# The up product of a gated feed-forward block by Strassen's scheme, on one Trainium2 core

## The chip, the cores and the metric

The kernel runs on one core of a Trainium2 chip. Its time is the device time of one execution in microseconds, given as the median of three runs. Five engines run side by side, each with its own instruction queue that it works off in order: TensorE (PE, with its weight loads as PEld), VectorE (DVE), ScalarE (ACT), GpSimd (POOL) and SyncE (SP, which here only issues DMAs). They meet in semaphores.

## The reference, cut to what matters

A trunk of two layers is applied to two sequences (prompt and sample) of 256 tokens, width 1024, in float32. Each layer has an attention mixer with two kinds of heads, a layer norm, and then the part that is changed, a gated feed-forward block with a convolution along the tokens:

```python
def conv_glu(x, w_up, conv_w, conv_b, w_down):      # D_FF = 2816, w_up: 1024 x 5632
    S = x.shape[1]
    g, v = jnp.split(x @ w_up, 2, axis=-1)
    gp = jnp.pad(g, ((0, 0), (1, 1), (0, 0)))
    g = gp[:, :S] * conv_w[0] + gp[:, 1:S + 1] * conv_w[1] + gp[:, 2:S + 2] * conv_w[2] + conv_b
    return (jax.nn.gelu(g) * v) @ w_down

# in encoder_trunk, for each layer:
x = layer_norm(ALPHA * x + mix, ln1_g[i], ln1_b[i])
ffn = conv_glu(x, w_up[i], conv_w[i], conv_b[i], w_down[i])
gate = jax.nn.sigmoid(x @ w_ple_gate[i] + b_ple_gate[i])
x = layer_norm(ALPHA * x + ffn + gate * (p[i] @ w_ple[i]), ln2_g[i], ln2_b[i])
```

## The kernel before

All 512 tokens (256 of the prompt, then 256 of the sample) are held at once. To get float32 accuracy out of a matmul with shortened operands, every operand is split into a high part (a copy into the short format, by ScalarE) and a low part (the value minus its high part, by GpSimd for weights and by VectorE for activations), and each product is three matmuls, hi x hi, hi x lo and lo x hi, added up in PSUM (`product`, lines 1238 to 1242). Each matmul has its own weight load. PSUM is eight banks of 512 columns, `ps[:, bank, :]`.

Weights come as a stream of blocks of 128 x 1024. SP loads a block into one of two slots of `raw`; ScalarE writes `w_hi` (`hi`, line 646), GpSimd writes `w_lo` (`lo`, line 535), in a ring of eight slots; TensorE uses it. SP may load the next block into a raw slot when GpSimd has finished with it (`w_split`), and ScalarE may overwrite a slot of the ring when TensorE has used it (`w_used`).

Around the change a layer goes as follows. The gate product (`w_ple_gate`, eight groups of 24 matmuls) ends; then TensorE runs the up loop. Its 22 tiles are of 128 gate and 128 value columns of `w_up` each. For a tile, `up_tile` runs the gate half and then the value half, 8 k-steps x 3 matmuls with 512 token columns each, into two banks:

```python
for v in range(2):
    pe.wait_ge(w_split.sem, w_split.at(layer, s[0] + v - AHEAD + 1) + s[1])
    a = slot(s[0] + v, KD)
    for k in range(KD):
        ins = product(ps[:, bank + v, :], (a[0][:, k, :], a[1][:, k, :]), (xt_hi[:, k, :], xt_lo[:, k, :]),
                      k == 0, k == KD - 1)
```

Behind it ScalarE takes the centre tap of the convolution (`conv_centre`, line 756), VectorE adds the two side taps (`conv_sides`, lines 1120 and 1123), ScalarE applies GELU (line 762) and VectorE multiplies with the value half (`glu`, line 1129). The result goes to `hbuf` (16 tiles) or `late` (the last six, split into `s_hi` and `s_lo` at once, lines 853 and 1198). The first 16 tiles run in hardware loops on all engines (`Fori`), the last six are written out. Then the down product: its first group (tile 16) makes one block of 6 matmuls for each of the four token blocks, into the banks of `DOWN_BANK`, and the other tiles follow, with their split in step (lines 858 and 1202).

The order of the work on every engine is written out by hand; a waiting instruction holds everything behind it on its engine.

## Time and profile before

| | |
|---|---|
| median of three runs | 1203.26 us (1203.0 to 1203.35) |
| the profiled execution: span from first to last instruction | 1201.6 us |
| TensorE busy | 1187.7 us (99%), 5784 matmuls |
| weight loads busy | 972.2 us (81%) |
| VectorE, ScalarE, GpSimd busy | 522.3 us (43%), 483.7 us (40%), 585.3 us (49%) |
| mean granted clock of TensorE | 0.996 |
| DMA | 113.45 MB, 94 GB/s over the span |

The profiled execution's own time is its span and what lies around it; the median of the runs is 1.66 us above the span. Busy times of matmuls overlap, as one starts before the record of the one ahead of it ends, so the length of a stage is read from starts and not from the sum of the records.

### The profile page before, as it was taken

The numbers are of one execution on the slowest core, as the hardware profiler recorded it, in microseconds if no ns is written. First come the engines' busy times: TensorE is split into PE (matmuls) and PEld (weight loads), VectorE is DVE, ScalarE is ACT, GpSimd is POOL, SyncE is SP. The second block draws the span as 40 slices with busy tenths as digits, with TensorE's granted clock in tenths as the row PEclk, the third lists the DMA queues.
The fourth block names the chain that finished last, engine by engine and source line by source line (L and its number), as shares of the span: only waits on it lengthen the run. The fifth ranks groups of instructions, "written<-read, shape, count | busy, mean of one in ns | idle before, by whom it ended". The sixth has DMA issues, their size and how long they took to land.

```text
span 1201.6 us, 16482 instructions
## 1 busy us (share of the span) xinstructions
PE 1187.7 (99%) x5784; PEld 972.2 (81%) x5784; DVE 522.3 (43%) x1094; ACT 483.7 (40%) x890; POOL 585.3 (49%) x338
## 2 busy tenths in 40 slices
PE   8999999999999999999999999999999999999997
PEld 6887778888888888888888777788888888888886
DVE  7777857522122134211587787474221122441107
ACT  3456763344334333323144767433443333332310
POOL 6665854465444444344264756634644444434330
PEclk9999999999999999999999999999999999999999
DMA  6321222344323332223132202433433333223311
GB/s 224 87 78 46 89 59 100 127 135 124 105 87 89 103 106 90 86 93 104 53 88 71 81 26 71 140 105 88 140 109 101 103 89 99 94 75 101 105 35 70
DMA packets 121754, 113.45 MB, mean 94 GB/s; under 512 B 6753, under 2 KB 97889, under 8 KB 121697
## 3 DMA queue, kind: packets, MB, share of 16 engines
q1 hardware_dynamic: 121696, 112.71, 30.3%
q8 instruction: 33, 0.54, 0.2%
q14 instruction: 25, 0.20, 0.1%
HBM read 110.60 MB, written 2.10 MB: 94 GB/s over the span
## 4 chain that ended last, share of the span: by engine, by line
PE 97%; DVE 1%; POOL 1%; DMA 1%; DVEq 1%; issue 0%; SPq 0%
PE ps L1240 29%; PE ps L1241 29%; PE ps L1242 29%; PE ps L1406 3%; PE ps L1392 3%; PE ps L1380 1%; PE ps L1382 1%; PE ps L1250 1%; PE ps L1363 1%; DMA x<-in_x_prompt_dram 1%; POOL w_lo L545 1%; DVEq L887 0%; POOL ln_r L541 0%; PE ps L1417 0%; DVE bn L1222 0%; PE ps L1462 0%
## 5 line engine op out<-in xcount | busy, mean ns | idle before, releaser
L535 POOL TENSOR_TENSOR w_lo<-raw,w_hi 128x1024 fp32r<-128x1024 f32 x188 | 453.1, 2412 | 404.7 <-ACT w_hi L646 404.5
L1240 PE MATMUL ps<-xt_hi,w_hi 128*128 128x512 f32 x704 | 273.9, 389 | 0.0
L1241 PE MATMUL ps<-xt_lo,w_hi 128*128 128x512 f32 x704 | 273.9, 389 | 0.0
L1242 PE MATMUL ps<-xt_hi,w_lo 128*128 128x512 f32 x704 | 273.9, 389 | 0.0
L646 ACT ACTIVATE w_hi<-raw 128x1024 fp32r<-128x1024 f32 x188 | 197.8, 1055 | 132.6 <-PE ps L1242 63.0
L1240 PE MATMUL ps<-w_hi,stat 128*128 128x512 f32 x480 | 187.8, 391 | 0.0
L1241 PE MATMUL ps<-w_lo,stat 128*128 128x512 f32 x480 | 187.1, 390 | 0.0
L1242 PE MATMUL ps<-w_hi,stat 128*128 128x512 f32 x480 | 187.0, 390 | 0.0
L1240 PEld LDWEIGHTS ps<-xt_hi,w_hi 128*128 128x128 f32 x704 | 132.1, 188 | 27.7
L1242 PEld LDWEIGHTS ps<-xt_hi,w_lo 128*128 128x128 f32 x704 | 132.1, 188 | 27.4
L1241 PEld LDWEIGHTS ps<-xt_lo,w_hi 128*128 128x128 f32 x704 | 132.1, 188 | 27.2
L1240 PE MATMUL ps<-w_hi,xt_hi 128*128 128x512 f32 x352 | 141.5, 402 | 2.3 <-POOL w_lo L545 2.1
L1242 PE MATMUL ps<-w_hi,xt_lo 128*128 128x512 f32 x352 | 138.4, 393 | 0.0
L1241 PE MATMUL ps<-w_lo,xt_hi 128*128 128x512 f32 x352 | 138.1, 392 | 0.0
L1120 DVE SCALAR_TENSOR_TENSOR hbuf<-ps,cols,hbuf 128x510 f32 x32 | 24.0, 749 | 189.3 <-ACT hbuf L756 189.3
L1242 PEld LDWEIGHTS ps<-w_hi,stat 128*128 128x128 f32 x480 | 90.1, 188 | 19.2
L1240 PEld LDWEIGHTS ps<-w_hi,stat 128*128 128x128 f32 x480 | 90.1, 188 | 18.1 <-POOL w_lo L535 0.8
L1241 PEld LDWEIGHTS ps<-w_lo,stat 128*128 128x128 f32 x480 | 90.2, 188 | 17.1
L1202 DVE TENSOR_TENSOR stat<-hbuf,stat 128x512 fp32r<-128x512 f32 x32 | 22.2, 693 | 140.1 <-ACT stat L858 140.1
L1240 PEld LDWEIGHTS ps<-w_hi,xt_hi 128*128 128x128 f32 x352 | 66.6, 189 | 16.7 <-POOL w_lo L545 3.6
L1242 PEld LDWEIGHTS ps<-w_hi,xt_lo 128*128 128x128 f32 x352 | 66.4, 189 | 14.5
L1241 PEld LDWEIGHTS ps<-w_lo,xt_hi 128*128 128x128 f32 x352 | 66.6, 189 | 11.8
(123 smaller groups left out, 1322.2 us busy)
## 6 DMA issues: line engine op xcount, KB each, us to landing
raw<-in_w_up_dram SPq DMA_DIRECT2D x88, 512.0 KB, 3.8
raw<-in_w_down_dram SPq DMA_DIRECT2D x44, 512.0 KB, 3.2
raw<-in_w_in_dram SPq DMA_DIRECT2D x22, 512.0 KB, 3.8
raw<-in_w_out_dram SPq DMA_DIRECT2D x16, 512.0 KB, 3.3
raw<-in_w_ple_gate_dram SPq DMA_DIRECT2D x16, 512.0 KB, 3.3
scratch<-in_ln_g_dram SPq DMA_DIRECT2D x5, 512.0 KB, 4.5
scratch<-in_ln_b_dram SPq DMA_DIRECT2D x5, 512.0 KB, 6.2
raw<-in_w_ple_dram SPq DMA_DIRECT2D x4, 512.0 KB, 3.3
```

What stands on the lines that cost most here:

```text
L535: pool.tensor_tensor(w_lo[:, n, :], raw[:, n % RAW, :], w_hi[:, n, :].bitcast(F32), ALU.subtract).then_inc(w_split.sem, 1)
L545: pool.tensor_tensor(w_lo[:, s, :], first_raw(s), w_hi[:, s, :].bitcast(F32), ALU.subtract).then_inc(w_split.sem, 1)
L646: act.activation(w_hi[:, n, :], raw[:, n % RAW, :], ACT.Copy).then_inc(w_hi_done.sem, 1)
L1120: dve.scalar_tensor_tensor(out=d[:, :, 1:], in0=g[:, :, 0:SEQ - 1], scalar=conv_w[:, 0, bass.ds(j, 1)], in1=d[:, :, 1:], op0=ALU.mult, op1 ...
L1202: dve.tensor_tensor(s_lo[:, 6 + v % 2, :], hbuf[:, bass.ds(i * 8 + v, 1), :].rearrange("p a n -> p (a n)"), s_hi[:, 6 + v % 2, :].bitcast( ...
L1240: pe.matmul(out, a[0], b[0], start=first, stop=False)
L1241: pe.matmul(out, a[0], b[1], start=False, stop=False)
L1242: return pe.matmul(out, a[1], b[0], start=False, stop=last)
L1250: ins = pe.transpose(ps[:, TRB + b, k * P:(k + 1) * P], x[:, t, (4 * b + k) * P:(4 * b + k + 1) * P], ident[:, :])
L1363: ins = pe.transpose(ps[:, TRB + u % 2, k * P:(k + 1) * P], rot[:, t % 2, k * P:(k + 1) * P], ident[:, :])
L1392: ins = pe.transpose(ps[:, TRB + u % 2, kb * 256 + qt * P:kb * 256 + (qt + 1) * P], probs(g)[:, qt * 256 + kb * P:qt * 256 + (kb + 1) * P] ...
L1406: ins = pe.matmul(head_bank(j)[HD * odd:HD * odd + HD, :], vbuf[:, k, 2 * s + kb, b // 2 * HD:(b // 2 + 1) * HD], probs_t[:, (2 * j + odd) ...
```

## The change

Two gate/value column blocks (the upper and lower half of the 1024 rows of w_up for a gate tile and its value tile) and the two halves of the tokens (prompt and sample) form a 2 x 2 by 2 x 2 product. Instead of eight block products of 512 rows and 256 tokens, seven are run, in the form of Strassen's scheme with 15 sums. `up_phases` gives TensorE's order: for tile j p1, p2, p5, p6, then p3 and p4 of tile j-1, then p7 of tile j. Each is 4 k-steps x 3 matmuls with 256 token columns.

- The sums over tokens (t1 to t4) are formed once a layer, during the gate product, by VectorE (`t_add`, `t_low`) and ScalarE (`t_high`); for that ScalarE also keeps an unsplit copy of the turned activations (`x_raw`, `norm_hi` with `keep`).
- The sums over weight blocks are formed for each tile: `pair_sums` on VectorE makes the two corner differences (1024 columns, into `scratch`) and two more sums of 512 columns (into banks 4 and 5). The four operands are then split: `outer_hi`, `corner_hi`, `inner_hi`, `pure_hi` on ScalarE; the residuals of the first, second and fourth on GpSimd and of the third on VectorE (`inner_low`).
- Three partial results are copied out of PSUM by ScalarE (`snap` of p1 and p6, `snap_product` of p5, 256 columns each) and added by VectorE (`v_sum`, 256 columns, `g_sum`, 512).
- SP loads a gate block and a value block as a pair, alternately into `raw` and into a part of `stat`, two pairs ahead. The load of the norm's ln2 parameters moves from ahead of the up loop into the down product.
- The up loop and the first part of the down loop are written out on all engines. The order of the splits of tiles 16 to 21 for the down product changes (`REST_ORDER`), and in the first down group token block 0 now waits for the last inner residual and block 1 for tile 19 of h; block 2 waits for tile 20 and block 3 for tile 21 as before.

```diff
+UP_BANKS = ((2, 3), (6, 7), (0, 1))
+REST_ORDER = (0, 4, 5, 1, 2, 3)
...
+def up_phases():
+    order = []
+    for j in range(FT):
+        order += [("p1", j), ("p2", j), ("p5", j), ("p6", j)]
+        if j == FT - 1:
+            order += [("p3", j - 1), ("p7", j), ("p4", j - 1)]
+        else:
+            if j:
+                order += [("p3", j - 1), ("p4", j - 1)]
+            order.append(("p7", j))
+    order += [("p3", FT - 1), ("p4", FT - 1)]
+    a, b = order.index(("p7", 0)), order.index(("p1", 1))
+    order.insert(a, order.pop(b))
+    return order
...
# TensorE
+                def up_product(name, j):
+                    (part, at), side = FACTORS[name]
+                    n = up_place(layer, j, part)
+                    g, v = UP_BANKS[j % 3]
+                    bank, half = {"p2": (g, 0), "p5": (g, 1), "p3": (g, 1)}.get(name, (v, 0))
+                    out = ps[:, bank, half * SEQ:(half + 1) * SEQ]
+                    for k in range(4):
...
+                        pe.matmul(out, a[0], b[0], start=opens, stop=False, skip_group_check=True)
+                        pe.matmul(out, a[0], b[1], start=False, stop=False, skip_group_check=True)
+                        ins = pe.matmul(out, a[1], b[0], start=False, stop=k == 3, skip_group_check=True)
+                    ins.then_inc(phase_done.sem, 1)
...
+                for name, j in PHASES:
+                    if name == "p1":
+                        pe.wait_ge(pair_lo.sem, pair_lo.at(layer, 3 * j + 1))
...
+                    elif name == "p5":
+                        pe.wait_ge(pair_lo.sem, pair_lo.at(layer, 3 * j + 2))
+                    elif name == "p6":
+                        pe.wait_ge(inner_split.sem, inner_split.at(layer, j + 1))
+                        pe.wait_ge(snapped.sem, snapped.at(layer, 3 * j + 1))
+                    elif name == "p7":
+                        pe.wait_ge(snapped.sem, snapped.at(layer, 3 * j + 3))
+                    elif name == "p3":
+                        pe.wait_ge(snapped.sem, snapped.at(layer, 3 * j + 2))
+                    elif name == "p4":
+                        pe.wait_ge(pair_lo.sem, pair_lo.at(layer, 3 * j + 3))
+                        pe.wait_ge(v_summed.sem, v_summed.at(layer, j + 1))
...
# ScalarE, tile loop (j - 2, j - 1, j and j + 1 are in work at a time)
+                for j in range(FT + 1):
+                    if j >= 2:
+                        gelu(j - 2)
...
+                        snap(j, 0)
+                    if 0 < j < FT - 1:
+                        outer_hi(j + 1)
+                    if j < FT - 1:
+                        corner_hi(j + 1)
+                    if j == FT - 1:
+                        body_hi(DOWN_AT)
+                        act.wait_ge(pair_lo.sem, pair_lo.at(layer, 3 * (FT - 1)))
+                        rest_hi(0)
+                    if j < FT:
+                        snap_product(j)
+                        snap(j, 1)
+                    if j < FT - 1:
+                        inner_hi(j + 1)
+                    if j == FT - 1:
+                        body_hi(DOWN_AT + 1)
+                    if j == FT:
+                        looped_h(0)
+                    if j:
+                        conv_centre(j - 1)
+                    if j < FT - 1:
+                        pure_hi(j + 1)
+                    if j == FT - 1:
+                        body_hi(DOWN_AT + 2)
+                        body_hi(DOWN_AT + 3)
+                gelu(FT - 1)
...
# VectorE
+                def pair_sums(m):
...
+                    dve.tensor_tensor(scratch[:, 0:2, :], up_corners(m), up_block(m, 2).unsqueeze(1).to_broadcast([P, 2, 512]),
+                                      ALU.subtract).then_inc(pair_outer.sem, 1)
+                    dve.drain()
+                    dve.tensor_tensor(ps[:, 4, :], scratch[:, 1, :], up_block(m, 0), ALU.add)
+                    dve.drain()
+                    dve.tensor_tensor(ps[:, 5, :], up_block(m, 1), ps[:, 4, :], ALU.subtract).then_inc(pair_inner.sem, 1)
...
+                for j in range(FT + 1):
+                    if j:
+                        v_sum(j - 1)
+                    if j >= 2:
+                        glu(j - 2)
...
+                    if j < FT - 1:
+                        pair_sums(j + 1)
...
+                    if j:
+                        g_sum(j - 1)
+                    if j < FT - 1:
+                        inner_low(j + 1)
+                    if j:
+                        conv_sides(j - 1)
+                glu(FT - 1)
...
# GpSimd: three residuals a tile; SP: the down loads behind the last pair
+                sp.wait_ge(pair_inner.sem, pair_inner.at(layer, FT))
+                sp.wait_ge(pair_lo.sem, pair_lo.at(layer, 3 * FT))
+                for n in range(LOOPED + 1):
+                    if n >= RAW:
+                        raw_free(DOWN_AT + n)
+                    load(DOWN_AT + n, down_source(layer, n - 1 if n else LOOPED), 1)
...
# TensorE, first down group
-                    if t >= 2:
+                    if t == 0:
+                        pe.wait_ge(inner_split.sem, inner_split.at(layer, FT))
+                    else:
                         pe.wait_ge(h_done.sem, h_done.at(layer, FT - 3 + t))
```

## Rows read from the trace of the kernel before

**Rows 1.** The page's chain that ended last: shares of the span by engine.
```profile
PE 97%; DVE 1%; POOL 1%; DMA 1%; DVEq 1%; issue 0%; SPq 0%
```

**Rows 2.** First up loop by stretch: us, busy PE, PEld, DVE, ACT, POOL, clock, DMA.
```profile
246.90:486.60 239.70, 239.70 (x1059) 198.46 (x1059) 61.95 (x74) 90.53 (x104) 110.70 (x47) 1.00 0.35 103
```

**Rows 3.** Groups of TensorE instructions by shape: count, busy us, mean ns, idle before.
```profile
L1240 PE MATMUL ps<-xt_hi,w_hi 128*128 128x512 f32 x704 | 273.9, 389 | 0.0
L1380 PE MATMUL ps<-k_split,stat 128*128 128x256 f32 x128 | 38.3, 321 | 0.0
```

**Rows 4.** TensorE in order of time, a burst of scores: start us, length us, instruction.
```profile
111.58 0.28 PE L1382 MATMUL ps<-k_split,stat 128*128 128x256 f32 x1
111.70 0.28 PE L1380 MATMUL ps<-k_split,stat 128*128 128x256 f32 x1
111.82 0.28 PE L1382 MATMUL ps<-k_split,stat 128*128 128x256 f32 x1
111.94 0.39 PE L1240 MATMUL ps<-w_hi,stat 128*128 128x512 f32 x1
```

**Rows 5.** Groups of ScalarE instructions by shape.
```profile
L646 ACT ACTIVATE w_hi<-raw 128x1024 fp32r<-128x1024 f32 x188 | 197.8, 1055 | 132.6 <-PE ps L1242 63.0 <-DMA raw<-in_w_up_dram 40.6 <-DMA raw<-in_w_in_dram 11.6
L652 ACT ACTIVATE xt_hi<-ps 128x512 fp32r<-128x512 f32 x32 | 17.4, 595 | 50.6 <-PE ps L1250 50.6
L756 ACT ACTIVATE late<-ps,cols 128x512 f32<-128x512 f32 x12 | 9.4, 781 | 47.3 <-PE ps L1242 47.3
L762 ACT ACTIVATE late<-late 128x512 f32<-128x512 f32 x12 | 7.6, 632 | 11.2 <-DVE late L1123 11.2
```

**Rows 6.** Groups of VectorE instructions by shape.
```profile
L1086 DVE TENSOR_TENSOR ps<-x,ps 128x1024 f32<-128x1024 f32 x6 | 7.4, 1229 | 30.5 <-PE ps L1242 30.5
L1129 DVE TENSOR_TENSOR late<-late,ps 128x512 f32<-128x512 f32 x12 | 8.3, 688 | 36.1 <-PE ps L1242 36.1
L1120 DVE SCALAR_TENSOR_TENSOR late<-ps,cols,late 128x510 f32<-128x510 f32 x12 | 9.0, 749 | 32.7 <-ACT late L756 32.7
```

**Rows 7.** Groups of GpSimd instructions by shape.
```profile
L535 POOL TENSOR_TENSOR w_lo<-raw,w_hi 128x1024 fp32r<-128x1024 f32 x188 | 453.1, 2412 | 404.7 <-ACT w_hi L646 404.5
```

**Rows 8.** GpSimd and VectorE in order of time, near 433 us.
```profile
433.30 2.40 POOL L535 TENSOR_TENSOR w_lo<-raw,w_hi 128x1024 fp32r<-128x1024 f32 x1 [2.42 <-ACT w_hi L646]
433.78 2.48 DVE L1198 TENSOR_TENSOR stat<-late,stat 128x512 fp32r<-128x512 f32 x1 [0.98 <-ACT stat L853]
```

**Rows 9.** GpSimd and VectorE in order of time, 569 to 575 us.
```profile
569.86 2.47 POOL L535 TENSOR_TENSOR w_lo<-raw,w_hi 128x1024 fp32r<-128x1024 f32 x1 [3.05 <-ACT w_hi L646]
569.99 2.49 DVE L929 TENSOR_TENSOR rope_a<-rope_sb,late 128x128 f32<-128x128 f32 x1
572.29 2.44 POOL L535 TENSOR_TENSOR w_lo<-raw,w_hi 128x1024 fp32r<-128x1024 f32 x1
572.40 2.48 DVE L930 TENSOR_TENSOR rope_a<-rope_sb,late 128x128 f32<-128x128 f32 x1
```

**Rows 10.** ScalarE and VectorE in order of time, the taps of a written-out tile.
```profile
437.55 0.78 ACT L756 ACTIVATE late<-ps,cols 128x512 f32<-128x512 f32 x1 [3.80 <-PE ps L1242]
438.36 0.75 DVE L1120 SCALAR_TENSOR_TENSOR late<-ps,cols,late 128x510 f32<-128x510 f32 x1 [2.11 <-ACT late L756]
439.18 0.75 DVE L1123 SCALAR_TENSOR_TENSOR late<-ps,cols,late 128x510 f32<-128x510 f32 x1
440.05 0.63 ACT L762 ACTIVATE late<-late 128x512 f32<-128x512 f32 x1 [0.78 <-DVE late L1123]
```

**Rows 11.** The page's DMA issues: count, KB each, us from issue to landing.
```profile
raw<-in_w_down_dram SPq DMA_DIRECT2D x44, 512.0 KB, 3.2
```

**Rows 12.** Table by stretch, early in the span (columns as in group 2).
```profile
20.00:21.00 1.00, 0.00 (x0) 0.00 (x0) 1.00 (x3) 0.00 (x0) 1.00 (x1) 1.00 0.00 0
22.00:23.00 1.00, 1.00 (x4) 0.71 (x4) 0.93 (x3) 0.00 (x0) 1.00 (x1) 0.50 0.62 78
24.00:25.00 1.00, 1.00 (x4) 0.81 (x4) 0.79 (x1) 0.00 (x0) 1.00 (x1) 0.50 0.58 203
```

More of the change, by code:

```diff
@@ L557, in body_lo @@
                 def body_lo(s):
-                    lo(s % SLOTS, w_hi_done.at(layer, s - AHEAD + 1))
+                    lo(place(layer, s), s % RAW, w_hi_done.at(layer, s - AHEAD + 1))
                 def normalise(g):
@@ L641, in _, with norm_hi @@
         def _(act):
-            def hi(n, landed, used):
-                act.wait_ge(raw_landed[n % RAW].sem, landed)
-                act.wait_ge(w_used.sem, used)
-                act.activation(w_hi[:, n, :], raw[:, n % RAW, :], ACT.Copy).then_inc(w_hi_done.sem, 1)
-            def norm_hi(t, full):
+            def norm_hi(t, full, keep=False):
                 for b in range(2):
@@ new lines, in body_hi, with pair_free, outer_hi @@
+                    act.activation(w_hi[:, n, :], raw[:, b, :], ACT.Copy).then_inc(w_hi_done.sem, 1)
+                def pair_free(m, name, slots):
+                    if m >= 2:
+                        wait_phase(act, layer, name, m - 2)
+                    else:
+                        act.wait_ge(w_used.sem, w_used.at(layer, slots))
+                def outer_hi(m):
+                    n = up_place(layer, m, 0)
+                    act.wait_ge(pair_landed[m % 2].sem, pair_landed[m % 2].at(layer, 32 * (m // 2 + 1)))
+                    pair_free(m, "p2", GATE_AT + 4 + 4 * m)
+                    act.activation(w_hi[:, n, :], up_outer_rows(m), ACT.Copy).then_inc(pair_hi.sem, 1)
@@ new lines, in corner_hi, with inner_hi @@
+                def corner_hi(m):
+                    n = up_place(layer, m, 1)
+                    act.wait_ge(pair_outer.sem, pair_outer.at(layer, m + 1))
+                    pair_free(m, "p7", GATE_AT + 4 + 4 * m)
+                    act.activation(w_hi[:, n, :], sums, ACT.Copy).then_inc(pair_hi.sem, 1)
+                def inner_hi(m):
+                    n = up_place(layer, m, 2)
+                    act.wait_ge(pair_inner.sem, pair_inner.at(layer, m + 1))
+                    pair_free(m, "p3", GATE_AT + 4 + 4 * m)
+                    act.activation(w_hi[:, n, :], ps[:, 4:6, :].rearrange("p a n -> p (a n)"), ACT.Copy).then_inc(pair_hi.sem, 1)
@@ new lines, in snap, with snap_product @@
+                def snap(j, n):
+                    wait_phase(act, layer, ("p1", "p6")[n], j)
+                    if n == 0 and j >= 2:
+                        act.wait_ge(g_summed.sem, g_summed.at(layer, j - 1))
+                    act.activation(snaps(layer, j)[:, n * SEQ:(n + 1) * SEQ], ps[:, UP_BANKS[j % 3][1], 0:SEQ],
+                                   ACT.Copy).then_inc(snapped.sem, 1)
+                def snap_product(j):
+                    wait_phase(act, layer, "p5", j)
+                    if j >= 2:
+                        act.wait_ge(v_summed.sem, v_summed.at(layer, j - 1))
+                    act.activation(snap_five(layer, j), ps[:, UP_BANKS[j % 3][0], SEQ:TOK], ACT.Copy).then_inc(snapped.sem, 1)
@@ L1183, in _ @@
                     if q == 0:
[L1184 removed]
+                        norm_lo(3, xt_hi_done.at(layer, 11), layer)
                     gate_apply(*divmod(q, TT))
[L1187 to L1191 removed]
```

423 lines of the change are left out of this document (285 added, 138 removed).

## The prediction, made before the change was run

> **What bounds the kernel now.** I read the page's chain first: TensorE holds 97% of it [rows 1]. Then the table by stretch for the up loop of the first layer: TensorE busy for all of 239.70 us at full clock, with VectorE at 62, ScalarE at 91 and GpSimd at 111 us [rows 2]. The second layer's up loop is alike. The reader is to see there that nothing in this stage waits but the engines beside TensorE. A layer's up loop is 22 x 2 x 8 x 3 = 1056 matmuls; 239.70 us over the 1059 of the row is 0.2264 us each, start to start (the 0.389 us of a single record [rows 3] overlaps its neighbours and is not its price). So the stage costs 239.0 us a layer, 478 of the 1201.6 us span.
>
> **What the change does to TensorE.** Seven products of 4 k-steps x 3 matmuls, 256 columns wide, replace two tiles of 24 matmuls at 512 columns: 84 for 48. The price of a 256-wide matmul with its own weight load stands in the scores of attention, the only such matmuls on full 128x128 weights in this number format [rows 3]. In order of time they start at 111.58, 111.70, 111.82, and the next matmul at 111.94: 0.12 us each [rows 4]. Half of 0.2264 would be 0.113, so each matmul carries a fixed 0.013 us, and there are more of them now. A round is 84 x 0.12 = 10.08 us (before 48 x 0.2264 = 10.87); a layer 1848 x 0.12 = 221.8 us. That is 17.2 us saved a layer, if TensorE never waits. All the rest is about whether it does.
>
> The Trainium skill, "TensorE: Matmul & The Clock Gate", section "Back-to-back issue gap", gives 262 cycles for 256 columns and 518 for 512, at 2.4 GHz an estimated 0.109 and 0.216 us. The rows are slower for both forms. By the page the saving would be 1056 x 0.216 - 1848 x 0.109 = 26 us a layer (an estimate), but the chain laid out next, at 10.0 us a round, would then set the pace.
>
> **What it adds beside TensorE, round by round.** The sums over weight blocks, the splits, the copies out of the banks and the sums of products fall on engines that had room. ScalarE gets per round four splits (1.05, 1.05, about 1.0 and, like a GELU of that width, 0.63 us), three short copies (each under the 0.60 of a 512-wide one), the centre tap 0.78 and GELU 0.63: about 6.3 of 10.08 us [rows 5]. GpSimd gets two residuals of 2.41 us and a half one: about 6.0 [rows 7]. VectorE gets two operations of 1024 columns at 1.23, four of 512 at 0.69, one of 256 (0.42, carrying on the step from 1024 to 512) and the two side taps at 0.75: about 7.1 [rows 6]. No engine is full, but VectorE takes its work in order, and its round closes on itself: GELU of tile j-2, gating, weight sums of j+1, their residual, side taps of j-1, GELU of j-1. I lay this ring out from the start of a GELU, with hand-overs of 0.03 to 0.12 us and 0.07 behind a drain [rows 10]:
> - GELU 0.63 and gating 0.69: 1.36.
> - Corner differences, 1024 columns, both inputs in SBUF: starts a little before the gating's record ends, done at 2.50.
> - Next is a 512-wide sum, again with both inputs in SBUF. Such an operation and a GpSimd subtraction exclude each other: VectorE's took 2.48 us where 0.69 is usual, and ended 0.56 us behind GpSimd's end [rows 8]. ScalarE's split of the outer blocks follows the GELU and a short copy, so GpSimd asks at about 1.96, waits for the corners, and then needs 2.25, as the second residual of [rows 9] did from the end of the product that held it: to 4.75. The sum ends at 5.31.
> - The last sum reads PSUM and is free: 6.07. ScalarE's inner split out of PSUM (about 1.02, from two of 0.595 less one start [rows 5]): 7.13. VectorE's inner residual 1.23: 8.40 (the g sum fits into the gap before it; the centre tap runs beside it).
> - Side taps 2 x 0.75 with a drain: 9.89. To the next GELU 0.12: 10.0 us.
>
> So the ring is 10.0 us by rows against TensorE's round of 10.08. This near-tie is the weak spot. Waits on two semaphores, which these rows don't show by themselves, can add up to about 0.25; below, the ring can lose 2.3 us where GpSimd comes late and doesn't block the sum. I take 10.25. The ring may first drift a little: it is hung on the end of p3, at 5 x 1.44 = 7.2 us of the round, after which the g sum runs; so GELU starts near 1.2 us of the next round, and the copy of p1 behind it is done 0.93 later, at 2.1. TensorE needs it for p6 at 3 x 1.44 = 4.3 us. That is 2.1 us of drift at no cost: 22 x 0.17 - 2.1 = 1.6 us lost a layer.
>
> **Stage ends.** At the start, p7 of tile 0 needs the copy of p6, which ScalarE does behind the corner split of tile 1, itself behind t4's residual and the weight sums: about 0.7 us late. At the end, the four first down splits stand in ScalarE's queue ahead of GELU 20 and the centre tap of 21. Count from the end of the last product. Round 20 begins 16 products of 1.44 before it, its GELU 1.2 later, and the last pair's third residual ends 9.7 into that ring: near -12.2. That frees the raw slots. Two down loads are issued; one takes 3.2 us to land [rows 11], the second some 2 more. Splits and residuals follow in the two slots: first residual done -5.4, third load landed -2.0, second residual done -2.5 (a VectorE split, again two SBUF inputs, comes between), fourth load landed +0.8, its split +1.9. Then GELU 20 at 2.5, gating 3.2, a down split of VectorE that waits for GpSimd until 4.9, g sum 5.5, centre 6.3, side taps 7.9, GELU 8.6, gating of tile 21 at 9.3. TensorE has four blocks of 6 x 0.2264 = 1.36 us to do meanwhile; the fourth, at 4.1, needs tile 21: 5.3 us lost where the kernel before lost none. Bounds: 0, if the loads land early enough to leave the tail off, and about 9, if one of the two rounds of loads comes 4 us later than laid out. The crowding of these splits also makes p7 and p4 of tile 21 late by about 1.0 in all.
>
> TensorE's clock: after it had stood still for all of 20 to 21 us, the granted clock was at 0.50 (1.2 GHz of 2.4) in 22 to 23 us and still in 24 to 25 [rows 12]; some three us at half speed cost 1.5. After a stop of 5.3 us part of that falls into the stop itself: 0.8 a layer.
>
> The gate stage also gets work: eight copies on ScalarE (0.60 each), four sums and three residuals on VectorE (1.23 each) and the first pair. VectorE has 43 us of gate products for about 33 of work, and each gate needs only the sum of two gates before; I cost it at nothing, and up to 2 us if blocked operations pile up. With the loop written out, the reloads of activation tables inside it go, which were off the path. SP's loads now wait on weight sums a pair back and land some rounds early.
>
> **Sum.** Per layer: -17.2 + 0.7 + 1.6 (ring) + 1.0 (tile 21) + 5.3 + 0.8 = -7.8 us. Two layers: -15.6. The profiled execution has a span of 1201.6 us and the median is 1203.26, 1.66 us around it; 1201.6 - 15.6 + 1.66 = 1187.7. I say 1188; with the ring from 10.08 to 10.4 and the fourth block's wait from 3 to 7, 1178 to 1197.
>
> **Rivals.**
> - *All waits hidden*: the end of the stage finds its weights early, the ring stays under 10.08. 2 x 17.2 = 34.4 off: 1169. For it: DMA is busy a third of the time in this stage [rows 2]; against it: the two slots make each load wait for a residual.
> - *The ring sets the pace* (slower side): place, VectorE's order with its blocked sum; price (L - 10.08) x 22 - 2.1 a layer for a ring of L. It takes back the whole remaining gain of 9.4 at L = 10.60, six tenths above what the rows give. At L = 11 the loss is 18.1 less 9.4, or 8.7 a layer: 1221. For it: some twelve hand-overs in a row; 0.05 each would do it. Against: the rows' hand-overs are in the sum already.
> - *GpSimd keeps going first*: if the second residual also passed ahead of the waiting sum, the ring would grow by 2.3 to 12.3; (12.3 - 10.08) x 22 - 2.1 - 9.4 = 37.3 a layer: 1278. Against it stands one place of this trace: with two residuals back to back, the small VectorE product that had waited since 569.99 ended at 572.48, just behind the first, and the second residual took 2.44 instead of 2.40; only the next product waited for that one [rows 9]. The Trainium skill, "SBUF — State Buffer", section "Who interferes with whom", says that the order of issue decides who blocks; by that the waiting sum gets its turn, and the trace agrees.
> - *The burst price doesn't hold*: four matmuls in a row may be served from what the queue holds; 1848 in straight code need two instructions every 0.12 us. At 0.1242 us the forecast's gain is gone, at 0.13 the time is 1203 + 2 x (18.5 - 7.8) = 1225. For it: no long run of this form stands in the trace; against: the burst runs into the next 512-wide matmul without a slower step [rows 4].
>
> **Chances.** Forecast 0.50; all hidden 0.13; ring 0.20, half of it below break-even; GpSimd first 0.05; burst price 0.12, half of it slower. About 0.2% is what a measurement of this kernel can tell from no change. Faster: 0.50 + 0.13 + 0.07 + 0.04 = 0.74; within 0.05; slower 0.21. Range 1167 to 1216: from all hidden to a ring near 11; the forecast's own is 1178 to 1197.
>
> **What would show it.** Up matmuls 0.12 us apart inside a product. TensorE's wait for p6 and p7: none or some 0.2 us a round, released by ScalarE. The 512-wide weight sum at about 2.7 us instead of 0.69, ending half a us behind GpSimd's outer residual. One wait of about 5 us per layer at the fourth down block, released by VectorE's gating, and a dip of the granted clock there. Wrong, if the 256-wide step is over 0.124, if the sum ends behind GpSimd's second residual, or if rounds are longer than 10.6.

## The result, and the profile after

The changed kernel takes 1210.16 us (median of 4 runs, 1208.54 to 1211.91) against 1203.22 for the kernel before: a ratio of 1.0057, 95% interval 1.0043 to 1.0072. It is slower by 0.6%, where 1.3% faster was forecast. The profiled execution of the changed kernel took 1211.91 us, with a span of 1210.1 and a mean granted clock of 0.985.

The page's chain of what ended last, shares of the span by engine, answers to [rows 1]: TensorE's 97% have become 66%.

```profile
PE 66%; DVE 13%; DVEq 6%; ACT 5%; DMA 4%; POOL 3%; issue 2%; SPq 0%; ACTq 0%
```

From where the same matmul starts in both traces the lengths of the stages can be worked out (us; the first row counts from the span's start; "down" is the time of the first 120 matmuls of the down product, behind which both kernels run alike):

| stage | before | after | forecast of the difference |
|---|---|---|---|
| up to the first gate | 201.5 | 204.0 | none |
| gate, layers 0 and 1 | 45.4, 45.4 | 49.3, 49.1 | none (0 to 2) |
| up, layers 0 and 1 | 239.4, 239.4 | 226.2, 224.8 | -13.9 |
| down, layers 0 and 1 | 27.2, 27.2 | 42.0, 38.6 | +6.1 |

So the up loop gave what was forecast: 13.2 and 14.6 us, 27.8 in all. The down stages took back 26.2, the gate stages 7.6, and 2.5 were lost ahead of the first gate.

The table by stretch of the changed kernel (columns as in [rows 2]) shows the up loop of layer 0 from its second round to its last, then the start of the down product.

```profile
264.30:466.10 201.80, 201.80 (x1682) 201.66 (x1682) 175.06 (x178) 112.89 (x178) 140.79 (x61) 1.00 0.36 100
466.10:483.60 17.50, 13.75 (x98) 12.36 (x97) 7.17 (x10) 7.90 (x12) 8.88 (x4) 1.00 0.42 132
483.60:490.00 6.40, 1.79 (x7) 1.18 (x7) 4.44 (x5) 2.38 (x4) 1.10 (x1) 0.79 0.42 137
490.00:493.40 3.40, 3.40 (x8) 2.68 (x9) 1.51 (x1) 1.44 (x2) 3.35 (x2) 0.50 0.00 0
493.40:510.90 17.50, 16.29 (x70) 13.11 (x69) 6.49 (x4) 4.83 (x7) 6.66 (x3) 0.98 0.58 180
510.90:518.00 7.10, 4.05 (x11) 2.89 (x10) 6.12 (x4) 4.26 (x7) 4.71 (x2) 0.76 0.32 88
```

In the first line TensorE is busy without a gap: 201.80 us over 1682 matmuls are 0.12 us each, the price taken from the burst of [rows 4]. From the second line on it is not. The line from 490.00 to 493.40 is one to remember: TensorE is busy for all of it, and yet only 8 matmuls fit in, since the granted clock is 0.50.

Who let TensorE wait, over the whole changed kernel (total us, times, longest):

```profile
PE ps L1539 <- DVE scratch L1336: 12.4, 4, 4.6
PE ps L1539 <- DVE stat L1404: 5.3, 4, 3.0
PE ps L1539 <- DVE late L1309: 3.9, 2, 2.1
...
PE ps L1810 <- ACT w_lo_f L840: 2.5, 2, 1.7
```

The lines shown are, in this order, the gating of tiles 20 and 21 (L1336), the residual of the looped tiles of h (L1404, `looped_low`), the sum of a gate (L1309) and the copy of a product out of its bank (L840). Only the last, and of the first the part of tile 21, had been laid out. ScalarE in order of time (start us, length us, instruction, idle before and its releaser) shows what holds the gating at the end of layer 0's up loop:

```profile
470.43 1.06 ACT L797 ACTIVATE w_hi<-raw 128x1024 fp32r<-128x1024 f32 x1 [2.80 <-DMA raw<-in_w_down_dram]
...
478.20 1.06 ACT L797 ACTIVATE w_hi<-raw 128x1024 fp32r<-128x1024 f32 x1 [2.28 <-DMA raw<-in_w_down_dram]
481.19 1.06 ACT L797 ACTIVATE w_hi<-raw 128x1024 fp32r<-128x1024 f32 x1 [1.93 <-DMA raw<-in_w_down_dram]
482.15 0.61 ACT L950 ACTIVATE scratch<-scratch 128x512 f32<-128x512 f32 x1
...
485.89 0.78 ACT L943 ACTIVATE scratch<-ps,cols 128x512 f32<-128x512 f32 x1 [2.61 <-DVE ps L1350]
488.39 0.63 ACT L950 ACTIVATE scratch<-scratch 128x512 f32<-128x512 f32 x1 [1.72 <-DVE scratch L1330]
```

The third and fourth down split (478.20, 481.19) wait for their loads, and GELU 20 (482.15) stands behind them. GELU 21 starts at 488.39, tile 21 is gated behind it, and TensorE goes on at 489.87. Some microseconds later the same engine does it again, to the looped splits of h (L861):

```profile
495.99 1.06 ACT L797 ACTIVATE w_hi<-raw 128x1024 fp32r<-128x1024 f32 x1 [4.55 <-DMA raw<-in_w_down_dram]
496.95 0.61 ACT L861 ACTIVATE stat<-hbuf 128x512 fp32r<-128x512 f32 x1
...
510.27 1.06 ACT L797 ACTIVATE w_hi<-raw 128x1024 fp32r<-128x1024 f32 x1 [9.43 <-DMA raw<-in_w_down_dram]
511.24 0.61 ACT L861 ACTIVATE stat<-hbuf 128x512 fp32r<-128x512 f32 x1
```

And in the gate stage VectorE does it to the sum of gate 1 (L1309), which stands behind a residual that waits for ScalarE's kept copies and behind the first sum of token blocks (L1358); TensorE waits from 222.2 to 224.4 for it:

```profile
219.49 0.69 DVE L1112 TENSOR_TENSOR xt_lo<-ps,xt_hi 128x512 fp32r<-128x512 f32 x1 [4.11 <-ACT hbuf L768]
...
222.44 1.23 DVE L1358 TENSOR_TENSOR ps<-hbuf 128x1024 f32<-128x1024 f32 x1
223.58 0.69 DVE L1309 TENSOR_TENSOR late<-ps,late 128x512 f32<-128x512 f32 x1
```

### The profile page after: what moved, and what is told of

It is laid out like the page before. It is cut to its first block, busy times and chain, and to the rows that moved or that the text cites. A ratio compares the mean times of both kernels' runs of the same rounds, so it can differ in the third digit from the quotient of the medians.

```text
span 1210.1 us, 19482 instructions
## 1 busy us (share of the span) xinstructions
PE 1167.1 (96%) x7368; PEld 1026.0 (85%) x7368; DVE 828.4 (68%) x1374; ACT 580.6 (48%) x1120; POOL 680.4 (56%) x382
## 4 chain that ended last, share of the span: by engine, by line
PE 66%; DVE 13%; DVEq 6%; ACT 5%; DMA 4%; POOL 3%; issue 2%; SPq 0%; ACTq 0%
PE ps L1539 13%; PE ps L1540 13%; PE ps L1541 13%; PE ps L1810 6%; PE ps L1812 6%; PE ps L1811 6%; DVE ps L1383 5%; DMA raw<-in_w_down_dram 3%; DVEq L1382 3%; PE ps L1704 3%; PE ps L1690 3%; DVE w_lo L1391 2%; ACT w_hi L822 2%; POOL w_lo L648 2%; PE ps L1678 1%
## 5 line engine op out<-in xcount | busy, mean ns | idle before, releaser
L648 POOL TENSOR_TENSOR w_lo<-raw,w_hi 128x1024 fp32r<-128x1024 f32 x100 | 242.1, 2425 | 145.5 <-ACT w_hi L797 145.2
L1539 PE MATMUL ps<-w_hi,stat 128*128 128x512 f32 x480 | 191.4, 399 | 17.7 <-DVE scratch L1336 12.4
L1810 PE MATMUL ps<-xt_hi,w_hi 128*128 128x256 f32 x704 | 199.4, 283 | 1.7 <-DVE ps L1343 1.7
L1811 PE MATMUL ps<-xt_lo,w_hi 128*128 128x256 f32 x704 | 199.2, 283 | 0.0
L1812 PE MATMUL ps<-xt_hi,w_lo 128*128 128x256 f32 x704 | 199.2, 283 | 0.0
L1541 PE MATMUL ps<-w_hi,stat 128*128 128x512 f32 x480 | 189.3, 394 | 0.0
L1810 PE MATMUL ps<-stat,w_hi 128*128 128x256 f32 x528 | 150.0, 284 | 4.0 <-ACT w_lo_f L840 2.5
L1811 PE MATMUL ps<-stat,w_hi 128*128 128x256 f32 x528 | 149.4, 283 | 0.0
L1812 PE MATMUL ps<-stat,w_lo 128*128 128x256 f32 x528 | 149.4, 283 | 0.0
L797 ACT ACTIVATE w_hi<-raw 128x1024 fp32r<-128x1024 f32 x100 | 105.1, 1058 | 77.1 <-DMA raw<-in_w_down_dram 46.3
L739 POOL TENSOR_TENSOR w_lo<-scratch,w_hi 128x1024 fp32r<-128x1024 f32 x44 | 123.9, 2816 | 13.5 <-ACT w_hi L816 13.5
L1404 DVE TENSOR_TENSOR stat<-hbuf,stat 128x512 fp32r<-128x512 f32 x32 | 33.6, 1049 | 123.7 <-ACT stat L861 123.7
```

The source lines that it names most:

```text
L648: pool.tensor_tensor(w_lo[:, n, :], raw[:, b, :], w_hi[:, n, :].bitcast(F32), ALU.subtract).then_inc(w_split.sem, 1)
L739: pool.tensor_tensor(w_lo[:, corner, :], sums, w_hi[:, corner, :].bitcast(F32), ALU.subtract).then_inc(pair_lo.sem, 1)
L797: act.activation(w_hi[:, n, :], raw[:, b, :], ACT.Copy).then_inc(w_hi_done.sem, 1)
L1539: pe.matmul(out, a[0], b[0], start=first, stop=False)
L1541: return pe.matmul(out, a[1], b[0], start=False, stop=last)
L1810: pe.matmul(out, a[0], b[0], start=opens, stop=False, skip_group_check=True)
```

## The experiments

Theory: the up loop's gain is real, and it is given back by the order of the queues around it: work that waits stands ahead of work that TensorE needs, at the down start in ScalarE's queue, in SP's loads, and in VectorE's gate stage; the stops also bring the clock down. Rivals: the down weights are late by themselves (two raw slots); the clock falls whatever the order.

**Four splits moved.**

```diff
-                    if j == FT - 1:
-                        body_hi(DOWN_AT)
-                        act.wait_ge(pair_lo.sem, pair_lo.at(layer, 3 * (FT - 1)))
-                        rest_hi(0)
                     if j < FT:
                         snap_product(j)
                         snap(j, 1)
+                    if j == FT - 1:
+                        body_hi(DOWN_AT)
+                        act.wait_ge(pair_lo.sem, pair_lo.at(layer, 3 * (FT - 1)))
+                        rest_hi(0)
...
-                    if j == FT - 1:
-                        body_hi(DOWN_AT + 1)
                     if j == FT:
                         looped_h(0)
+                        body_hi(DOWN_AT + 2)
...
                     if j == FT - 1:
-                        body_hi(DOWN_AT + 2)
-                        body_hi(DOWN_AT + 3)
+                        body_hi(DOWN_AT + 1)
                 gelu(FT - 1)
+                body_hi(DOWN_AT + 3)
```

> Only ScalarE's order at the end of the up loop is changed: the first down weight is split behind the last copies of tile 21, the second behind the centre tap of tile 20, the third behind GELU 20, the fourth behind GELU 21. Theory (the four down splits stood in ScalarE's queue ahead of the work of tiles 20 and 21): TensorE's waits there, 2.0 + 1.1 + 1.6 + 5.0 us in layer 0 and 1.1 + 1.1 + 2.4 + 5.0 in layer 1, shrink to about 1 a layer, some 17 us in all; the clock's stretch at half speed at the start of the down product (6.8 and 10.2 us, worth 8.5 us) goes with them: about 1185. Rival A (the stops don't bring the clock down; it falls at the end of the up loop in any case): 1193. Rival B (the down weights come late by themselves, through two raw slots): the waits move to the later down blocks, 1204 or above.

Measured 1201.87 us, ratio 0.9985 (0.9976 to 0.9995): 8 us of the 25 that were expected. The waits for GELU went. A new one came, in both layers, ahead of the second looped block; this is TensorE's wait in layer 0, and ScalarE in order of time:

```profile
PE ps L1538 <- DVE stat L1403: 5.5, 1, 5.5
```

```profile
487.33 1.06 ACT L797 ACTIVATE w_hi<-raw 128x1024 fp32r<-128x1024 f32 x1 [3.97 <-DMA raw<-in_w_down_dram]
...
490.08 1.06 ACT L797 ACTIVATE w_hi<-raw 128x1024 fp32r<-128x1024 f32 x1 [1.17 <-DMA raw<-in_w_down_dram]
491.04 0.61 ACT L861 ACTIVATE stat<-hbuf 128x512 fp32r<-128x512 f32 x1
```

The looped split at 491.04 needs nothing that is late; two weight splits that wait for their loads, for 3.97 and 1.17 us, stand ahead of it. Rival B had said that the waits move on, but whether the loads or the order is to blame isn't told by this run.

**All splits later.** The same, and each later weight split two blocks further back:

```diff
-                body_hi(DOWN_AT + 4)
-                body_hi(DOWN_AT + 5)
                 for v in range(LOOPED):
...
-                    body_hi(DOWN_AT + 6 + v)
+                    body_hi(DOWN_AT + 4 + v)
+                body_hi(DOWN_AT + 20)
+                body_hi(DOWN_AT + 21)
```

> ScalarE's order alone again: the first four down splits as in the run that moved only these, and each later one two blocks later, so that no split that waits for its load stands ahead of the looped split that the next block needs. SP's queue and the gate stage are as in the changed kernel. Theory (what kept the wait of 5.9 us there was the splits of the fifth and sixth down weight, ahead of the second looped split in ScalarE's queue): the down stage loses about 2.4 + 1.1 us a layer and nothing else, the gain load behind the eighth down load costs nothing any more, and the clock stays up there: 1210 - 13.4 - 8.6 = 1188. Rival A (the gain load delays the down loads by itself): up to 6.7 us a layer remains, 1193 to 1200. Rival B (the loads are late through the two raw slots): 1200 or above.

Measured 1185.21 us, ratio 0.9852 (0.9835 to 0.9868), against 1188 expected. The down stages took 27.3 and 28.1 us, where the kernel before took 27.2. TensorE's waits from 465 to 540 us are down to one, the last up product's:

```profile
PE ps L1809 <- DVE ps L1342: 2.8, 1, 2.8
```

Loads, raw slots and SP's queue are those of the changed kernel. So the loads were early enough, and rivals A and B fall. ScalarE's order alone gave back 14.7 and 10.5 us of the two down stages. The up loops' ends took 3.0 of it, with 3.4 us at half speed behind the wait above, and the other 4.2 of the 26.4 us between the two profiled spans lie ahead of the first gate and in the gate stages, where this run changes nothing and the clock fell less.

**The gain load later.**

```diff
-                    if n == 7:
+                    if n == 12:
 
                         sp.wait_ge(h_rest_split.sem, h_rest_split.at(layer, 3))
                         sp.dma_start(ln_g, bcast(ln2_g
```

> Only SP's queue is changed: the load of the second norm's gains, which waits for three residuals of the last tiles, stands behind the 13th down load instead of the 8th. Theory (the down loads were held behind that wait and behind its two 512 KB transfers, and through ScalarE's splits the looped splits of h were too): TensorE's two waits of 1.6 and 3.4 us on the looped residual in layer 0 and 0.9 and 1.0 in layer 1 go, and the 3.4 us at half speed behind the second of them: 6 to 8.5 us less, 1202 to 1204. Rival (the loads are late through the two raw slots alone): under 2 us less, 1208 to 1210.

Measured 1202.15 us, ratio 0.9991 (0.9981 to 1.0), in the range of the theory. In layer 0 the down stage went from 42.0 to 35.7 us: the second of the two stretches at half speed is gone there, and the wait for looped residuals shrank from 4.3 us to this, while the one for tile 21's gating stayed:

```profile
PE ps L1539 <- DVE scratch L1336: 4.6, 1, 4.6
...
PE ps L1539 <- DVE stat L1404: 0.5, 1, 0.5
```

In layer 1 little changed: 37.7 us instead of 38.6, with 0.7 of the 1.1 us of that wait left.

The load of the gains did hold the down loads; but in the run with all splits later it stands where the change put it and costs nothing. It did harm only through the splits in ScalarE's queue.

**Gate sums first.**

```diff
-                    gate_sum(*divmod(q, TT))
+                    if q not in (1, 2):
+                        gate_sum(*divmod(q, TT))
                     if q == 0:
+                        gate_sum(0, 1)
                         norm_lo(3, xt_hi_done.at(layer, 11), layer)
                     gate_apply(*divmod(q, TT))
                     if q == 0:
+                        dve.drain()
+                        gate_sum(0, 2)
                         t_add(1)
```

> Only VectorE's order in the gate stage is changed: the sums of gates 1 and 2 stand ahead of the residual of the norm's fourth tile and of the first sum of token blocks. Theory (the fourth gate waited 2.2 us a layer for the sum of the second, which stood behind that residual, waiting for ScalarE's kept copies): both waits go, 4.3 us, and the 3.4 us at half speed behind each, 3.4 in all: 1202.5. Rival A (the clock falls there in any case): 1206. Rival B (the wait only moves on to a later gate, since VectorE has the same work): 1208 to 1212.

Measured 1207.38 us, ratio 1.0008 (0.9976 to 1.004), and 1197.22 to 1208.97 over six runs: as a time it settles nothing. The trace does for its stage: the gate stages take 45.8 and 45.4 us and the clock stays at 1.00, from 200 to 250 us with TensorE busy for 49.90 of 50.00. Of these 3.5 us a layer the up loop's start took back 0.9 and 2.1 (226.2 and 224.8 became 227.1 and 226.9), mostly because the second pair's outer residual is late now (0.9 us in each layer). And layer 1's down stage, still in the changed kernel's order, took 41.9 us in this execution instead of 38.6, with 4.0 us of waits for looped residuals where the changed kernel has 1.1 there.

**All three orders** (the splits of both runs, the gain load, the gate sums):

> The three changes of order together; besides, each down weight from the fifth on is split two blocks later, so that the looped splits of h don't stand behind a split that waits for its load. Theory: all that was given back outside the up loop returns, and what is left is the up loop's own 27.6 us less about 1 us at each up start and some 1 to 2 us at each down start: 1172 to 1180, faster than both kernels. Rivals: if the clock falls anyway, 1186; if the down weights are late by themselves, above 1195.

Measured 1181.34 us, ratio 0.9812 (0.9796 to 0.9829): faster than both kernels, 1.3 us above the top of what was expected. In the profiled execution the up loops won 25.5 us instead of 27.6, with waits of 2.3 us at the last up product and of 2.1 us in all at each up start, which had not been taken along.

**The clock's share.** The changed kernel, with products of zeros to fill the stop:

```diff
                     else:
+                        if t == TT - 1:
+                            for _ in range(20):
+                                pe.matmul(ps[:, DOWN_BANK[0], :], masks[:, 0, :], masks[:, :, :].rearrange("p a n -> p (a n)"),
+                                          start=False, stop=False, skip_group_check=True)
                         pe.wait_ge(h_done.sem, h_done.at(layer, FT - 3 + t))
```

> The changed kernel, with 20 products of zeros (512 columns, added to an open sum) put into the 5.0 us for which TensorE waits ahead of the fourth block of the first down group. Nothing else comes earlier. Theory (the stop brings the clock down, and that costs as much again): the waits stay, the stretch at half speed behind this stop (6.8 us in layer 0, 10.2 in layer 1) goes or shrinks, 3.4 + 5.1 = 8.5 us less: about 1201.5. Rival A (the clock falls for another reason, the smaller stops around it or the change of the matmul's width): 1209 to 1212. Rival B (the price of the clock is small, since part of the half-speed stretch lies in the stop): 1206 to 1209.

Measured 1209.31 us, ratio 1.0051 (1.0038 to 1.0065), not to be told from the changed kernel. The table by stretch shows why, in layer 0 and, in the last line, in layer 1:

```profile
486.50:490.00 3.50, 3.35 (x14) 2.74 (x15) 1.62 (x2) 1.72 (x3) 3.17 (x2) 1.00 0.00 0
490.00:493.40 3.40, 3.40 (x16) 2.82 (x15) 0.00 (x0) 0.63 (x1) 2.04 (x1) 1.00 0.60 171
493.40:497.00 3.60, 0.53 (x3) 0.15 (x2) 2.62 (x2) 2.88 (x5) 2.63 (x2) 1.00 0.34 130
...
1070.70:1074.10 3.40, 3.16 (x9) 1.33 (x9) 2.48 (x4) 0.78 (x1) 0.15 (x1) 0.50 0.50 154
```

In layer 0 the clock stays at 1.00 behind the filled stop, and by the end of the first looped block TensorE has gained 1.9 us on the changed kernel, counted from the stop. Then it stands before the next looped residual, which hangs on a load; the clock falls behind that stop, and the gain is gone (3.5 us are lost there). A later stop of 3.2 us of the changed kernel does not come, though, so that the first 120 matmuls are 4.3 us shorter in the end. In layer 1 the clock falls ahead of the filling already, behind the third block's stop of 2.1 us, and is at 0.50 for 3.4 us, where the changed kernel has 10.2; 1.7 us are gained, 1.4 of them are lost at the next residual, and with one more stop of 2.1 us the 120 matmuls are 1.3 us longer. So in layer 0 the stop of 5 us brought the clock down, which the theory says, and in layer 1 a shorter one ahead of it did. That this made the kernel as much longer again is not shown, because later waits were in its way.

**A stop alone**, in a kernel in which nothing else waits there (the tidied kernel below, with two long copies ahead of the ninth looped split):

```diff
                         act.wait_ge(w_used.sem, w_used.at(layer, DOWN_AT + v))
+                    if v == 8:
+                        for out in (xt_hi, xt_lo):
+                            act.activation(out[:, :, :], hbuf[:, 0:8, :], ACT.Copy)
```

> The same kernel with one stop put into the middle of each layer's down product, where no other wait follows: ScalarE makes two copies of 4096 columns (about 4 us each, into tiles that nothing reads any more) ahead of the ninth looped split of h. TensorE stops there for some 4 to 5 us a layer. Theory (a stop of this length brings the clock to half speed behind it): each stop costs its own length and 1.7 to 3.4 us more: 9 + 3.4 to 6.8 us in all above the kernel without it. Rival (a stop costs its length): 9 us, and no row at half speed behind it.

Measured 1188.14 us (1185.21 to 1190.01) against 1175.89 without the stops: 12.3 us. The profiled execution is the shortest of these. TensorE stood 3.2 us in each layer. These are the 3.4 us from the stop's start, and those that follow, in layer 0 and then in layer 1:

```profile
522.30:525.80 3.50, 0.47 (x4) 0.05 (x2) 0.69 (x1) 3.50 (x3) 0.00 (x0) 1.00 0.00 0
525.80:529.20 3.40, 3.40 (x15) 2.81 (x16) 2.48 (x1) 1.62 (x3) 3.17 (x2) 1.00 0.02 5
1099.80:1103.20 3.40, 0.41 (x2) 0.00 (x0) 0.69 (x1) 3.40 (x3) 0.00 (x0) 1.00 0.00 0
1103.20:1106.60 3.40, 3.36 (x11) 2.66 (x12) 2.47 (x1) 1.68 (x3) 3.12 (x2) 0.71 0.02 5
1106.60:1110.00 3.40, 3.40 (x14) 2.73 (x13) 0.00 (x0) 0.00 (x0) 2.06 (x1) 0.79 0.65 169
```

The same stop left the clock alone in layer 0 and brought it down for 3.4 us in layer 1; the down stage grew by 3.3 us there and 4.9 here. So a stop costs its length, and where the clock falls 1.7 us on top; neither theory nor rival holds in both layers. The medians are further apart than 6.4 us of stops and twice 1.7, by 2.5 us. The mean granted clocks point to where these lie: 0.996 in the profiled execution (1185.21 us), 0.991 in the two longest (1190.01 and 1189.54). A clock lower by 0.005 over 1188 us is about 5.9 us of work lost (an estimate), so it probably fell behind more stops there; no trace shows it.

**A longer ring.** The last weight sum of each pair is done twice, in the kernel with all three orders:

```diff
-                    dve.tensor_tensor(ps[:, 5, :], up_block(m, 1), ps[:, 4, :], ALU.subtract).then_inc(pair_inner.sem, 1)
+                    dve.tensor_tensor(ps[:, 5, :], up_block(m, 1), ps[:, 4, :], ALU.subtract)
+                    dve.drain()
+                    dve.tensor_tensor(ps[:, 5, :], up_block(m, 1), ps[:, 4, :], ALU.subtract).then_inc(pair_inner.sem, 1)
```

> The version with all three orders changed, and the last 512-wide weight sum of each pair done twice (0.70 us and a drain, some 0.76 us more in VectorE's round). Theory of the near-tie (GELU to GELU takes 10.07 us beside 10.08 of TensorE, with some 2.1 us to drift in): the ring becomes 10.83 and sets the pace, (10.83 - 10.08) x 22 - 2.1 = 14.4 us a layer: 1181 + 29 = 1210. Rival (the ring only follows TensorE and has room, as 10.07 beside 10.08 may mean): 1181 to 1185.

Measured 1214.41 us, ratio 1.009 (1.0073 to 1.0107): 33.1 us above the kernel without it, 4 more than expected, since hardly any drift came free: the up loops grew by 17.0 and 15.9 us, where 22 x 0.76 is 16.7. The rounds are 10.84 us:

```profile
304.91:315.75 10.84, 10.31 (x85) 10.13 (x85) 9.52 (x11) 5.67 (x10) 7.00 (x3) 1.00 0.36 99
315.75:326.59 10.84, 10.31 (x85) 10.13 (x85) 9.53 (x11) 5.67 (x10) 7.00 (x3) 1.00 0.35 96
```

The ring grew by 0.76 and every round by as much. So the ring of the change has no room: it is the near-tie that was laid out.

**Ends tidied.** Four more moves in the kernel with all three orders:

```diff
+                outer_hi(1)
+                t_high(4)
                 gate(1, 2)
                 gate(1, 3)
...
+                    if j == FT - 1:
+                        act.wait_ge(pair_lo.sem, pair_lo.at(layer, 3 * (FT - 1)))
+                        rest_hi(0)
                     if j < FT:
                         snap_product(j)
                         snap(j, 1)
                     if j == FT - 1:
                         body_hi(DOWN_AT)
-                        act.wait_ge(pair_lo.sem, pair_lo.at(layer, 3 * (FT - 1)))
-                        rest_hi(0)
```

(t4's residual goes ahead of the last gate's sum, too.)

> The version with all three orders changed, and four more moves: the split of the first left-over tile of h ahead of the last copies (its residual was held 2.4 us behind GpSimd's down residual, and the g sum and the v sum of the last tiles behind it), and the outer split of the second pair and the split of t4 ahead of the last two gates' tanh, with t4's residual on VectorE ahead of the last gate. Theory: the wait of 2.4 us at the last up product, most of the 1.1 us at the third down block, and the 1.0 and 1.3 us at the start of the up loop go: 4.5 to 5.5 us a layer, 1170 to 1173. Rival (the last tile's chain is as long as what hides it, and the up start waits for the corner's residual instead): 2 us a layer, 1177 to 1181.

Measured 1182.91 us, ratio 0.9823 (0.9806 to 0.9839): nothing won. The tails did get shorter, with one wait of 1.0 and 1.2 us left; but at the up start one of 3.5 us appeared. A gate's tanh now stood behind the second pair's outer split and t4's split, and the first of these waited 4.81 us for the end of the gate product:

```profile
250.06 1.06 ACT L810 ACTIVATE w_hi<-raw 128x1024 fp32r<-128x1024 f32 x1 [4.81 <-PE ps L1543]
251.02 1.01 ACT L833 ACTIVATE xt_hi<-ps 128x1024 fp32r<-128x1024 f32 x1
251.93 0.62 ACT L938 ACTIVATE late<-late 128x512 f32<-128x512 f32 x1
```

It is the fault of the change once more, made by me.

**Both ends.** The tail's move kept, and at the up start:

```diff
                 gate(1, 2)
+                outer_hi(1)
                 gate(1, 3)
...
                     if j == 0:
-                        outer_hi(1)
                         snap(0, 0)
                         t_high(4)
+                        snap_product(0)
+                        snap(0, 1)
```

> The version with all three orders changed, with the split of the first left-over tile of h ahead of the last copies (as in the run before), and at the start of the up loop: the outer split of the second pair between the last two gates' tanh, and tile 0's copies ahead of the second pair's corner split; t4's split stays behind the last tanh. Theory (the tail moves won 2 us a layer; the loss of 3.75 us at the up start came from a tanh queued behind t4's split, which waited for the end of the gate stage): 2.0 us at each tail and about 1.2 us at each start go, 1181.3 - 6.4 = 1175. Rival (the up start's chain through the second pair's corner residual is the limit whatever stands first): 1177 to 1178.

Measured 1175.89 us, ratio 0.9769 (0.9752 to 0.9785): 28 us faster than the kernel before (1203.65 in the runs beside it), 34 faster than the change as it was made. Stages: gate 45.7 and 45.4, up 223.6 twice, down 29.0 and 28.7. In the profiled execution the clock stays up from 20 to 1165 us, and in layer 0 two waits of over 0.3 us are left from 200 to 560 us:

```profile
20.00:1165.00 1145.00, 1136.41 (x7200) 1003.75 (x7201) 800.07 (x1346) 574.74 (x1111) 666.44 (x362) 1.00 0.32 94
```

```profile
PE ps L1545 <- DVE scratch L1338: 1.4, 1, 1.4
PE ps L1816 <- POOL w_lo L739: 1.0, 1, 1.0
```

## Why the prediction was wrong

**Right: the up product.** 0.12 us a matmul, with 10.08 us a round, held over the whole loop. The Trainium skill's figure ("TensorE: Matmul & The Clock Gate", section "Back-to-back issue gap"; an estimated 0.109 us, given there for a matmul by itself) was not reached in any round here; the measurement decides.

**Right: the ring**, nearly to the tenth. In the changed kernel GELU starts follow each other by (375.4 - 335.1) / 4 = 10.07 us:

```profile
L950 ACT ACTIVATE hbuf<-hbuf x5: 632/632/633, 335.1 to 375.4; 128x512 f32<-128x512 f32 x5
```

One ring in order of time, from the gating on:

```profile
356.02 0.69 DVE L1336 TENSOR_TENSOR hbuf<-hbuf,ps 128x512 f32<-128x512 f32 x1 [0.51 <-ACT hbuf L950]
356.62 1.22 DVE L1380 TENSOR_TENSOR scratch<-raw 128x1024 f32<-128x1024 f32 x1
357.21 2.89 POOL L736 TENSOR_TENSOR w_lo<-raw,w_hi 128x1024 fp32r<-128x1024 f32 x1 [2.24 <-ACT w_hi L810]
357.93 2.73 DVE L1383 TENSOR_TENSOR ps<-scratch,raw 128x512 f32<-128x512 f32 x1
360.06 2.85 POOL L739 TENSOR_TENSOR w_lo<-scratch,w_hi 128x1024 fp32r<-128x1024 f32 x1
```

The blocked sum took 2.73 us where 0.69 is usual [rows 6], and ended at 360.66, 0.56 behind GpSimd's first residual, as in [rows 8]; the second residual didn't pass it. That settles the rival of GpSimd going first, and the Trainium skill's rule on who blocks whom ("SBUF — State Buffer", section "Who interferes with whom") agrees. I had added 0.25 us a round for unseen waits; hardly any of it was there, and the ring's term of 1.6 us was nought. The longer ring shows how little there was to spare.

That the up stage as a whole came out as forecast (13.9 us a layer; 13.2 and 14.6 measured) is luck in part: its waits at the start and at tile 21 came to 4.0 and 3.1 us where 0.7 + 1.0 had been put, and stand in the place of the ring's term.

**Right in itself: the fourth block's wait**, 5.3 us forecast, 4.8 measured in each layer (a step of 4.99 us less a matmul's 0.23). The third block's wait, below, belongs to the same tail: with it TensorE stood 6.1 and 6.9 us for it.

**Wrong: what follows it.** The step that failed is "Stage ends", with "One wait of about 5 us per layer at the fourth down block": the count was ended at tile 21's gating. Three things lay beyond or beside it.
- ScalarE's queue behind the fourth block. I had listed the four down splits ahead of GELU 20, but not the later ones ahead of the looped splits of h. With the waits for loads they stopped TensorE for 1.4 and 3.2 us more in layer 0, and 0.7 twice in layer 1. GELU 20 came later than laid out, too, and the third block was stopped by 1.3 and 2.2 us; by the layout's own numbers tile 20's gating, at 3.2, already came after that block's turn at 2.7, and the sum has no term for it. The run with all splits later puts this order at 25.2 us of the down stages, with its waits and its clock.
- SP's gain load, moved between the down loads, where it waits for residuals of the last tiles and sends two transfers of 512 KB. The prediction doesn't mention it. Moving it away brought 8 us while the splits stood as they were (7.3 in the down stages of the profiled executions, 6.4 of them in layer 0). With the splits shifted the down stages are short although it stands where it was.
- The gate stage, "at nothing, and up to 2 us": 3.9 and 3.7 us. The balance of 33 us of work in 43 (VectorE was busy for 36.9 us of 45.4 in the run with the gate sums first) was beside the point, because the sum that the fourth gate needs stood behind a residual with a wait of 4.11 us.

**Mis-sized: the clock**, 0.8 us a layer. The profiled execution of the changed kernel spent 3.4 us at half speed behind each gate stop and 10.2 us in each down stage, some 27 us in all (the four lines from 483.60 to 518.00 of the first table give the 10.2 of layer 0: twice what each lacks to 1.00, times its length). TensorE stood still for 7.3 of them, 2.6 and 4.7 us in the two stops ahead of the fourth block, so that some 10 us of work were lost, 5 a layer.

One more such stretch, of 6.8 us near the start, has nothing to do with the change. Behind a stop that ends near 21.5 us and is alike in all twelve profiled kernels the clock fell in seven, for 3.4 or 6.8 us, and not in five. From 26 to 40 us the kernels before and after are alike, and show 75 and 65 matmuls:

```profile
26.00:40.00 14.00, 14.00 (x75) 11.80 (x74) 11.31 (x24) 7.16 (x13) 10.44 (x5) 1.00 0.35 99
```

```profile
26.00:40.00 14.00, 14.00 (x65) 11.75 (x64) 10.04 (x21) 6.77 (x11) 8.25 (x5) 0.86 0.39 106
```

The kernel with both ends tidied has 76 there, at 1.00.

So none of the rivals came true, and none of the three signs of being wrong showed, since all three look inside the loop. The upper end of the range, 1216, was worked out for a slower ring that didn't come (and by the prediction's own price a ring of 11 makes 1221); that the time lies below it is luck. The mechanism of the loop was right, and the loss came from outside it: the stages on either side were the place, and their price was put at 6.1 us a layer (5.3 + 0.8) where it was 18.7 and 15.1 with the gate stage. By the steps of the matmuls the down stages' 14.8 and 11.4 us are 10.7 and 8.3 of stops and 4.2 and 3.1 of slower matmuls. What stays open is what the time would be with these stops and an unbroken clock: the filled stop kept the clock up behind it in layer 0, but later waits took part of the gain back.

## What to carry to other kernels

When a stage is made shorter, lay out each engine's queue across both of its ends until everything is as early as it was before, not only until the first late item: with queues in order, an instruction that waits for a load costs whatever stands behind it. A balance of busy time over a stage (33 us of work in 43) says nothing of that; ask for each result that the bottleneck engine needs what stands ahead of it and what that waits for. And a loss at a stage's end may be mere order: here 34 us came back without one operation less.

## What the runs showed of the hardware

- Stops of TensorE of 2 to 5.7 us were mostly, not always, followed by 3.4 to 10.2 us at a granted clock of 0.50 (of the 10.2, 4.7 lay in the next stop). The same 3.2 us stop did it in one layer and not in the other, and the same stop near 21 us in seven of twelve kernels.
- Zero products in a stop of layer 0 kept the clock at 1.00 behind it: 16 matmuls of 512 columns in 3.4 us, where 8 had run. In layer 1 the clock had fallen ahead of them.
- Between two GpSimd subtractions back to back, a waiting VectorE sum of two SBUF inputs went first, in 40 of the changed kernel's 44 rounds; in the other four no subtraction ran beside it.
